# Stick-breaking attention on 127-key blocks, with carried sums and packed score products

## The reference, cut to what matters

```python
z = einsum('bqhd,bkhd->bhqk', q_blk, kh) * Dh ** -0.5
mask = key_pos[None, :] < q_pos[:, None]
log_1m_beta = where(mask, log_sigmoid(-z), 0.0)
between = cumsum(log_1m_beta, axis=3, reverse=True) - log_1m_beta
weights = where(mask, exp(log_sigmoid(z) + between), 0.0)
out = einsum('bhqk,bkhd->bqhd', weights, vh)
```

## Time and profile before

| what | value |
|---|---|
| median of three runs | 1556.13 us |
| the profiled execution | 1550.32 us, span 1548.5 us |
| TensorE busy | 1466.1 us (95%), 11281 matmul records |
| VectorE, ScalarE, GpSimd busy | 670.5, 525.2, 308.9 us (43%, 34%, 20%) |
| granted TensorE clock | 0.9 or more of full speed in all of 40 slices |
| DMA | 124.10 MB, 80 GB/s in the mean |

### The profile page before, as it was taken

How to read it: one execution, slowest core, us unless ns; L and a number is a source line. 1 busy time by engine, 2 the same in 40 slices (tenths; PEclk the granted TensorE clock), 3 DMA queues, 4 the chain that set the end, 5 groups by cost and what they waited for, 6 DMA issues and landing times.

```text
span 1548.5 us, 27297 instructions
## 1 busy us (share of the span) xinstructions
PE 1466.1 (95%) x11281; PEld 1138.3 (74%) x11281; DVE 670.5 (43%) x1072; ACT 525.2 (34%) x947; POOL 308.9 (20%) x412
## 2 busy tenths in 40 slices
PE   7989989989898899999999999999999999999997
PEld 5767777767677555554777788888888888888876
DVE  6244151555653454655464424242332424242337
ACT  5423231433323476877443403021120403021132
POOL 6674615422332252523001000000000000000000
PEclk9999989999999999999999999999999999999999
DMA  6454413423224513021433302021120302111014
GB/s 201 138 149 120 127 42 97 125 59 86 70 68 109 166 25 78 6 76 62 163 109 109 109 0 95 14 68 41 38 70 0 98 10 75 34 57 51 27 60 171
DMA packets 134969, 124.10 MB, mean 80 GB/s; under 512 B 20829, under 2 KB 112154, under 8 KB 134874
## 3 DMA queue, kind: packets, MB, share of 16 engines
q1 hardware_dynamic: 88588, 92.90, 19.4%
q10 hardware_dynamic: 46286, 29.84, 6.8%
HBM read 97.88 MB, written 24.84 MB: 79 GB/s over the span
## 4 chain that ended last, share of the span: by engine, by line
PE 47%; DVE 2%; ACT 1%; DMA 1%; issue 1%; POOLq 0%; SPq 0%; DVEq 0%; ACTq 0%
PE all_ps_b L2018 22%; PE all_ps_b L1995 22%; PE all_ps_b L1585 2%; DMA bk_acc<-in_w_out 1%; POOLq L1605 0%; DVE bk_acc L1872 0%; PE all_ps_b L1988 0%; ACT bk_acc L1773 0%; DVE bk_acc L1882 0%; DVE bk_w1L L1843 0%; DVE bk_acc L1868 0%; DVE all_hL L1888 0%; DVE all_gL L1914 0%; ACT bk_rect L1804 0%; DVE bk_acc L1945 0%
## 5 line engine op out<-in xcount | busy, mean ns | idle before, releaser
L1924 DVE TENSOR_TENSOR bk_acc<-bk_acc,all_ps_b 128x512 f32<-128x512 f32 x128 | 87.9, 687 | 274.4 <-PE all_ps_b L2018 274.2
L1995 PE MATMUL all_ps_b<-all_hH,bk_w1L 128*128 128x512 f32 x512 | 200.2, 391 | 5.1 <-PE all_ps_b L2018 2.1
L2018 PE MATMUL all_ps_b<-bk_w2H,all_gL 128*128 128x512 f32 x512 | 199.4, 389 | 2.5 <-DVE all_gL L1914 2.5
L1995 PE MATMUL all_ps_b<-all_hH,bk_w1H 128*128 128x512 f32 x512 | 199.4, 389 | 0.0
L1995 PE MATMUL all_ps_b<-all_hL,bk_w1H 128*128 128x512 f32 x512 | 199.3, 389 | 0.0
L2018 PE MATMUL all_ps_b<-bk_w2L,all_gH 128*128 128x512 f32 x512 | 199.2, 389 | 0.0
L2018 PE MATMUL all_ps_b<-bk_w2H,all_gH 128*128 128x512 f32 x512 | 199.2, 389 | 0.0
L1207 PE MATMUL fr_ps_F<-fr_hH,fr_wL 128*128 128x512 f32 (+1 forms) x416 | 174.7, 420 | 6.5 <-POOL fr_wL L459 6.4
L459 POOL TENSOR_TENSOR fr_wL<-fr_raw,fr_wH 128x256 fp32r<-128x256 f32 (+1 forms) x208 | 161.9, 809 | 26.0 <-ACT fr_wH L504 22.7
L1207 PE MATMUL fr_ps_F<-fr_hL,fr_wH 128*128 128x512 f32 (+1 forms) x416 | 164.8, 396 | 0.0
L1207 PE MATMUL fr_ps_F<-fr_hH,fr_wH 128*128 128x512 f32 (+1 forms) x416 | 164.5, 395 | 0.0
(11 more groups left out here) (349 smaller groups left out, 2281.9 us busy)
## 6 DMA issues: line engine op xcount, KB each, us to landing
fr_raw<-in_w_in ACTq DMA_DIRECT2D x37, 512.0 KB, 4.2
bk_raw<-in_w_ff SPq DMA_DIRECT2D x32, 512.0 KB, 4.3
all_raw<-in_w_ff SPq DMA_DIRECT2D x32, 512.0 KB, 3.7
projected<-fr_stage ACTq DMA_DIRECT2D x39, 256.0 KB, 4.4
fr_raw<-in_w_in SPq DMA_DIRECT2D x13, 512.0 KB, 4.3
fr_xt<-in_x SPq DMA_DIRECT2D x8, 512.0 KB, 5.1
bk_acc<-in_x SPq DMA_DIRECT2D x8, 512.0 KB, 3.3
x_after_mixers<-bk_acc SPq DMA_DIRECT2D x8, 512.0 KB, 2.6
```

The costliest lines, as they stand in the source:

```text
L1924: dve.tensor_tensor(acc[:, j, ds], acc[:, j, ds], ybank[g % 4][:], ALU.add).then_inc(collected, 1)
L1995: m = pe.matmul(bank[s][h][:], w[s][:, k, :], a[:, k, hs], start=(k == 0 and q == 0), stop=(k == KB - 1 and q == 2))
L2018: m = pe.matmul(ybank[g % 4][:], a[:, i, ts], w[:, i, ds], start=(i == 0 and q == 0), stop=(i == FB - 1 and q == 2))
```

## The change

- Blocks have 127 keys (`KEYS`) on rows 1 to 127. Row 0 of a block's scores is zero (its key and value columns are blank), row 0 of its softplus is overwritten with the sum over all later keys, and the triangle (`later`) has +1 in that row, so that the same matmul that subtracts the block's later keys adds the carried sum, and its own row 0 comes out as the carry for the next block. The all-ones product and GpSimd's running sum R are gone. Where queries have no later block yet, `later_only` ignores row 0.
- The carry goes from PSUM by a one-row copy on VectorE (`hand_on`) into `row`, and from there by a one-row copy on GpSimd into row 0 of the next step's E, after its softplus.
- Scores are one float32 matmul per head over 64 rows, the two heads in rows 0 to 63 and 64 to 127 of the array, in two PSUM banks. The splits of q and k, in `front` and in `heads`, are gone, and with them the double copies; q is scaled as it is stored in `front`. The mask product is float32.
- The two heads go in one step. A pair has 14 steps: 5 for the first query half (4, 131, 258, 385 and 512 queries wide) and 9 for the second (8, 135, 262, 389 and five times 512).
- k, v and q of a pair have two sets of buffers; k and v are loaded in runs of 127 keys. The output product's raw buffers are their own.
- The masks are made in `front`. The slots of GLA and of the output's pieces are counted anew (`GLA_AT`, `LAG` 28 for 26, `SPLIT_AT` and others), GLA's two pieces per step only in steps that aren't the first of their half.

```diff
-SB_MASKS = ("ones", "to_diag", "above", "same64")
+SB_MASKS = ("same64", "never", "later", "later_only")
...
-        self.qd, self.kd = [r.sb(f"qd{h}", [P, T]) for h in range(2)], [r.sb(f"kd{h}", [P, T]) for h in range(2)]
-        self.vp = r.sb("vp", [P, T])
-        self.kS = [r.sb(f"kS{h}", [P, T], F32R) for h in range(2)]
-        self.qH, self.qL = [[r.sb(f"{n}{h}", [P, T], F32R) for h in range(2)] for n in ("qH", "qL")]
+        self.k, self.v, self.q = [], [], []
+        for n in range(2):
+            self.k.append(r.sb(f"k{n}", [P, KCOLS]))
+            self.v.append(r.sb(f"v{n}", [P, KCOLS]))
+            self.q.append(r.sb(f"q{n}", [P, T]))
+        self.raw = [r.sb(f"raw{n}", [P, T]) for n in range(4)]
+        self.size = 4 * KCOLS + 2 * T + 4 * T
+    def load(self, q, proj, i, done):
+        n = i % 2
+        whole = TB * KEYS
+        for to, at in ((self.k[n], SB_K + i * P), (self.v[n], SB_V + i * P)):
+            q.dma_start(to[:, 0:TB * P].rearrange("p (b c) -> p b c", c=P)[:, :, 1:P],
+                        proj[at:at + P, 0:whole].rearrange("p (b c) -> p b c", c=KEYS)).then_inc(done, 16)
+            q.dma_start(to[:, TB * P + 1:TB * P + 1 + T - whole], proj[at:at + P, whole:T]).then_inc(done, 16)
+        q.dma_start(self.q[n][:], proj[SB_Q + i * P:SB_Q + (i + 1) * P, :]).then_inc(done, 16)
...
                 q.wait_ge(s(f"stored{b}"), 16 * stores(b, HALF_BLOCKS + NRW + SB_BLOCKS))
-            for h in range(2):
-                for part in range(2):
-                    rows_ = slice(C * part, C * part + C)
-                    q.dma_start(e.kd[h][rows_, :], proj[SB_K + C * h:SB_K + C * h + C, :]).then_inc(s("early_in"), 16)
-                    q.dma_start(e.qd[h][rows_, :], proj[SB_Q + C * h:SB_Q + C * h + C, :]).then_inc(s("early_in"), 16)
-            q.dma_start(e.vp[:], proj[SB_V:SB_V + P, :]).then_inc(s("early_v"), 16)
+            e.load(q, proj, 0, s("early_in"))
...
-                    act.copy(stage[b][0:wd, :], F[b][0:wd, :]).then_inc(s(f"taken{b}"), 1)
+                    act.activation(stage[b][0:wd, :], F[b][0:wd, :], ACT.Copy, scale=C ** -0.5 if at < SB_K else 1.0
...
-                for n, name in enumerate(SB_MASKS):
-                    const(lambda: dve.tensor_copy(con["sb_masks"][:, n, :], full[name]))
+                same64, never, later, later_only = [con["sb_masks"][:, n, :] for n in range(len(SB_MASKS))]
+                const(lambda: dve.tensor_copy(same64, full["same64"]))
+                const(lambda: dve.tensor_scalar(never, full["above"], -1.0, FAR, ALU.add, ALU.mult))
+                for to in (later, later_only):
+                    const(lambda: dve.tensor_scalar(to, full["to_diag"], -1.0, None, ALU.mult))
+                const(lambda: dve.memset(never[0:1, :], 0.0))
+                const(lambda: dve.memset(later[0:1, :], 1.0))
+                const(lambda: dve.memset(later_only[0:1, :], 0.0))
...
-            def early_key(h):
-                dve.wait_ge(s("early_high"), 2 * h + 1)
-                dve.tensor_tensor(e.kS[h][C:P, :], e.kd[h][C:P, :], e.kS[h][C:P, :].bitcast(F32), ALU.subtract)
-            def early_query(h):
-                dve.wait_ge(s("early_high"), 2 * h + 2)
-                dve.scalar_tensor_tensor(e.qL[h][:], e.qd[h][:], C ** -0.5, e.qH[h][:].bitcast(F32), ALU.mult, ALU.subtract)
             centre(LAST)
-            early_key(0)
             variance(LAST)
-            early_query(0)
             normed(LAST)
-            early_key(1)
-            early_query(1)
             gated(LAST)
...
-    UNITS = []
+    STEPS = []
     for c in range(QC):
-        for kb in range(PER * (c + 1) - 1, -1, -1):
-            for h in range(2):
-                UNITS.append((h, c, kb, max(0, (kb - PER * c) * P), kb == PER * (c + 1) - 1))
-    NU = len(UNITS)
-    NV = NU // 2
-    NZ, AHEAD = 4, 3
+        top = ((c + 1) * HALF - 1) // KEYS
+        for b in range(top, -1, -1):
+            STEPS.append((c, b, max(0, KEYS * b - c * HALF), min(P, (c + 1) * HALF - KEYS * b + 1), b == top))
+    NS = len(STEPS)
+    END = [max(n for n, x in enumerate(STEPS) if x[0] == c) + 1 for c in range(QC)]
+    ALL = PAIRS * NS
+    GLA_AT = [sum(2 for x in STEPS[0:n] if not x[4]) for n in range(NS + 1)]
+    TURNS = (range(1, 5), range(5, 9), range(0, 1))
+    VALUES_READY = [1 + max([n for n in range(3) if any(x[1] in TURNS[n] for x in STEPS[0:m + 1])]) for m in range(NS)]
+    def carries(S):
...
+        SQUARE_AT, SUM_AT, ROOT_AT = (None, 7, 2), (None, (8, 9), (3, 4)), (None, (9, 10), (4, 5))
+        SCALE_AT, HIGH_AT, LOW_AT = (None, 11, 6), (None, 11, 7), (None, 12, 8)
+        TURN_AT = ((1, 3), (9, 10, 11), (11, 12, 13))
+        SPLIT_AT = 6
+        GH, DK, DV, CH, NL, LAG = 4, 32, 64, HALF // C, 6, 28
...
+                    sp.wait_ge(s("z"), 2 * NS * (i - 1))
+                    sp.wait_ge(s("v_mm"), 3 * (i - 1))
+                early.load(sp, proj, i, s("in_qkv"))
...
-            sp.wait_ge(s("k"), LAST * 2)
-            sp.wait_ge(s("q"), LAST * 2)
...
-                units(i)
+            for S in range(ALL):
+                i, m, c, b, off, rows, first = at(S)
+                for h in range(2):
+                    if not first:
+                        known = at(S - 1)[4]
+                        pool.wait_ge(s("handed"), carries(S - 1) + h + 1)
+                        pool.wait_ge(s("sp"), 2 * S + h + 1)
+                        pool.tensor_copy(E[ring(S, h)][0:1, known:HALF], row[ring(S - 1, h)][0:1, known:HALF]
+                                         ).then_inc(s("placed"), 1)
+                        gla(i * GLA_AT[NS] + GLA_AT[m] + h - 1)
...
+            def exponential(S, h):
+                act.wait_ge(s("z"), 2 * S + h + 1)
+                if S >= 2:
+                    act.wait_ge(s("tri_mm"), 2 * (S - 2) + h + 1)
+                n = ring(S, h)
+                act.activation(part(E[n], S), part(Z[n], S), ACT.Exp).then_inc(s("exp"), 1)
+            def logarithm(S, h):
+                act.wait_ge(s("exp"), 2 * S + h + 1)
+                n = ring(S, h)
+                act.activation(part(E[n], S), part(E[n], S), ACT.Ln, bias=1.0).then_inc(s("log"), 1)
+            def weight(S, h):
+                act.wait_ge(s("tri_mm"), 2 * S + h + 1)
+                if S >= 2:
+                    act.wait_ge(s("v_mul"), S - 1)
+                if S < LAST_STEP and not at(S + 1)[6]:
+                    act.wait_ge(s("handed"), carries(S) + h + 1)
+                n = ring(S, h)
+                act.activation(part(W[n], S), part(Z[n], S), ACT.Exp).then_inc(s("weight"), 1)
...
+            for h in range(2):
+                logarithm(0, h)
+            for S in range(ALL):
+                i, m, c, b, off, rows, first = at(S)
+                if S < LAST_STEP:
+                    for h in range(2):
+                        exponential(S + 1, h)
+                    logarithm(S + 1, 0)
+                for h in range(2):
+                    weight(S, h)
+                if S < LAST_STEP:
+                    logarithm(S + 1, 1)
+                if i == LAST and m == SPLIT_AT:
+                    act.wait_ge(s("g_stored"), 32 * NH)
+                if i == LAST and m >= SPLIT_AT:
+                    for n in range(2 * (m - SPLIT_AT), min(2 * (m - SPLIT_AT) + 2, len(ahead.pieces))):
+                        ahead.split_high(act, n)
...
+            def softplus(S, h):
+                n = ring(S, h)
+                dve.wait_ge(s("log"), 2 * S + h + 1)
+                dve.scalar_tensor_tensor(part(E[n], S), part(E[n], S), CAP, part(Z[n], S), ALU.min, ALU.max
+                                         ).then_inc(s("sp"), 1)
+            def hand_on(S, h):
+                off = at(S)[4]
+                dve.wait_ge(s("tri_mm"), 2 * S + h + 1)
+                if S >= 2 and not at(S - 1)[6]:
+                    dve.wait_ge(s("placed"), carries(S - 2) + h + 1)
+                n = ring(S, h)
+                dve.tensor_copy(row[n][0:1, off:HALF], Z[n][0:1, off:HALF]).then_inc(s("handed"), 1)
+            for h in range(2):
+                softplus(0, h)
+            take_values(0, 0)
+            for S in range(ALL):
+                i, m, c, b, off, rows, first = at(S)
+                if S < LAST_STEP and not at(S + 1)[6]:
+                    for h in range(2):
+                        hand_on(S, h)
+                for h in range(2):
+                    if S < LAST_STEP:
+                        softplus(S + 1, h)
...
-                pe.matmul(Z[u % NZ][:, span(u)], kS[h][:, kb * P:(kb + 1) * P], qL[h][:, qs], start=True, stop=False)
-                m = pe.matmul(Z[u % NZ][:, span(u)], kS[h][:, kb * P:(kb + 1) * P], qH[h][:, qs], start=False, stop=True)
-                if kb >= PER * c:
-                    if not i and u == 0:
-                        pe.wait_ge(s("far"), 1)
-                    m = pe.matmul(Z[u % NZ][:, off:off + P], unit[:], never[:], start=False, stop=True,
```

(77 more changed lines are left out.)

297 lines of the change are left out of this document (79 added, 218 removed).

## The result

The change made the kernel slower: 1581.11 us in the median of four runs (1577.48 to 1584.67) against 1556.0, a ratio of 1.0161 (95% interval 1.0138 to 1.0185), 25 us. I had forecast 8. The profiled execution took 1581.12 us, its span is 1579.2. The attention stage alone has moved.

What follows compares the result with a forecast made beforehand. TensorE was taken to bound the attention stage (200.2 of 206.8 us busy). Chains and kept work, 187.5, plus 28 of waits give 215.5, 8.7 more; less 0.9 in front, 1550.32 becomes 1558.1 us (1564 against the median), range 1539 to 1586.

Steps and rivals of the forecast that it cites:

- My stage: Attention stage, first key sum to last values: 187.5 us plus 28 of queue waits, 215.5 against 206.8 before.
- the 83% that I gave for TensorE: Sign of being right: TensorE's busy share in the attention stage falls from 97% to near 83%.
- a clock below 0.95, which none of this counts: Sign of being wrong: a granted clock under 0.95, which no term of the forecast priced.
- Part (a): TensorE waits for ScalarE's GLA piece of the same step (kv, level product, sums): 0.9 to 1.6 us, six times, 7.6.
- (c): Outputs of the previous pair, value copies and their exponentials, queued in the attention stage: 6.5 us.
- where two fall into the same step only the longer counts: Rule for overlapping queue waits in the attention stage, by which their 34 us were taken as 28.
- The free full step: Steps 512 queries wide without GLA: 4.4 us by copy, exponential, scores, sums; 4.3 by the second chain through logarithm and softplus.
- Part (b): VectorE's GLA pieces between and behind its copies and softplus overrun the step: 15 us over both halves.
- (d): Last pair: two splits a step before the next copy, 3 us, and the split's wait for GLA stores, about 2.
- rival C: Score products' row halves don't run side by side, scores cost 0.85 more at full width: 1584 us; chance 0.14.
- B: Rival: TensorE stays the bound, queue waits fall into slack with six us remaining: 1542 us; chance 0.27.
- D: Rival: no difference, VectorE's one-row copy costs 0.3 us instead of 0.68, 1554 to 1556 us; chance 0.10.

Runs made afterwards that it cites:

- experiment 2: Changed kernel with TensorE multiplying into an unused bank in ten steps where it stood idle, and twice at the end of `front`: 1570.05 us.
- experiment 1: Changed kernel with ScalarE taking both logarithms of the next step before the two weights: 1578.75 us.
- experiment 6: Kernel before with packed float32 scores in row halves, both heads issued together two units ahead instead of three, blocks of 128 keys kept: 1566.33 us.
- experiments 3 and 7: The first has its own line; the second adds to it VectorE's GLA pieces behind both softplus and two multiplications at the end of `front`: 1551.27 us.
- experiment 5: Kernel of experiment 1 with the one-row copy reading zeros in SBUF, carried sum left out, weights not waiting for the copy: 1566.72 us.
- experiment 3: Kernel of experiment 1 with the first of ScalarE's two GLA pieces of a step moved before the weights: 1555.15 us.

## Why the prediction was right and wrong

**The mechanism was right, the clock failed.** My stage was 215.5 us; by the 83% that I gave for TensorE, 179 of it were work and 36.5 idle time; it became 239.0 with 41.2 and 197.8. The idle time was 5 short, the work 19. The step that failed is in the sum itself: "a clock below 0.95, which none of this counts". I priced each wait at its length and left the clock at nothing, without a reason. Over the program it went from 0.983 to 0.9745, and 0.0085 of 1581 us is 13, an estimate; with the clock held (experiment 2) 11 came back, net of the matmuls that held it. With my 8 the 13 are 21 of the 25. I had the rows to doubt it: the kernel before is not free of it either, its own median lies 6 us over the profiled execution, whose clock was 0.987.

**Part (a), 7.6 us, was 11.4 as waits** and 23.6 as a time won when it was undone. The places were right (kv, level, sums), five of the six that I had. The lengths were not: four of them were 1.81 to 3.70 us, for which I had 0.9 to 1.6. The 3.70 at 662.39 has 1.7 us of the previous pair's normalisation in front, which I had in (c) and took to be covered. So "where two fall into the same step only the longer counts" was wrong there: in one queue they add. The 2.44 and 2.23 of the first pair (557.89, 566.42) have no normalisation before them; the second head's logarithm stands there between weight and piece.

**The free full step.** The chain copy, weight, scores, sums at 4.4 us was right (4.53 once it stood alone), but it didn't bind. The second, at 4.3, did, with 4.97: I hadn't put the logarithm behind the weight in ScalarE's queue, took a sum's pitch (0.85) for its latency (1.07), left out the links, and GpSimd's copy takes 0.93 and not 0.65 while VectorE works (0.60 while it doesn't, 750.51). It cost little (experiment 1: 2 us) as the clock took back what the step gave.

**Part (b), 15 us, was too high as far as it was undone.** Undoing it where it stood between the softplus brought 4 us, and none once (a) was gone. The steps with the gated results, which that edit leaves as they are, made TensorE wait 2.50 and 2.29 us (scores at 620.59 and 720.26), for which I had 2 to 3 each. **(d)**: two waits behind the splits are 2.23 and 1.04 (728.84, 740.61), for which I had 3 in all, and 2 for the stores, which nobody waited for.

**TensorE's terms held.** The row halves run side by side: four records of scores, 1.06 us from start to the next load, where I had 1.06 with the switch and rival C 1.91. C, 1584, was near the time for the wrong reason. The ratio of the Trainium skill (TensorE: Matmul & The Clock Gate, Part 3) gave an estimate of 1.11 for a pair before the switch; the trace shows 1.06 with it, so two row halves overlap better here than that ratio of four smaller tiles. A third switch cost 0.12 us in a free pair of units (experiment 6), not 0.22, if the products themselves take the same time there. The one-row copies took 0.675 and 0.688 in the mean, for 0.68 and 0.65. The loads were waited for once, by a weight load, 1.4 us; the matmul behind it stood 0.56 idle (594.50). The stage behind stayed within 0.5 us; the front was 2.0 us shorter and not 0.9, in one execution of each.

**The other rivals.** B, that the waits fall into slack, is refuted by the change. The kernels of experiments 3 and 7 come nearer to it, with no difference from the kernel before that stands out of the noise and with 0.35% less, but neither reaches its 1542. D fell: the copy wasn't cheap, and without it (experiment 5) the time still was 0.6% over before.

Not settled: why the clock falls at the entry in some kernels and not in others with the same idle time (1.98 us in the kernel before, without a fall, 1.99 in experiment 6, with one), where the last 4 of the 25 us are, and what part of the 17 us of waits for weights is VectorE's.

## What to carry to other kernels

A wait of an engine that was the bound is priced with what it does to the clock: here each us of TensorE's idle time that one queue order made went with two to three more at 1.2 GHz (7 and 17 us in experiment 3). So when a change trades TensorE's work for waits, first look where the waits of 2 us stand, and repair the queue order there before judging the idea: the change as it was lost 1.6%, with two instructions' places in ScalarE's queue changed it lost nothing, and with VectorE's order and two useless matmuls besides it won 0.35%. A shorter lookahead with paired scores, and the same products, cost 0.7%.

## What the runs showed of the hardware

In the changed kernel the clock fell to 1.2 GHz after idle times of TensorE of 2.2 to 3.7 us, though not after each (2.29 at 720.26 left it at 2.4), and stayed there for 4 to 14 us, with TensorE busy for nearly all of the two stretches shown; useless float32 matmuls in the idle places kept it at 2.4 GHz and took 11 us off the time. A copy of one row of 512 took VectorE 0.68 us from PSUM and 0.41 from SBUF, and GpSimd 0.60 alone and 0.93 beside VectorE's work. Two heads' float32 products over 64 rows with 512 columns took 1.06 us to the next load, a switch of shape included, where one product over 128 rows takes 0.85 by its pitch.
